# A decoder step with paged attention: weights turned and values issued one group later, maxima behind all four key pairs, two buffers for a sequence's values

## The reference

```python
ckv_past = cache_ckv[l, page_table].reshape(db, past_len, KV_LORA)
kr_past = cache_krope[l, page_table].reshape(db, past_len, MLA_ROPE)
...
s_past = (jnp.einsum('bthl,bpl->bhtp', q_lat, ckv_past)
          + jnp.einsum('bthr,bpr->bhtp', q_rope, krope_past))
...
p = jax.nn.softmax(s, axis=-1)
lat = (jnp.einsum('bhtp,bpl->bthl', p[..., :P], ckv_past)
       + jnp.einsum('bhts,bsl->bthl', p[..., P:], c_kv))
return jnp.einsum('bthl,lhv->bthv', lat, w_uv)
```

## Time and profile before

| | us |
|---|---|
| timed runs, median of 3 | 1979.57 |
| lowest, highest | 1977.12, 1981.09 |
| span of the profiled execution | 1973.4 |
| PE busy in it | 1875.2 (95%) |
| DVE, ACT, POOL busy | 1215.5, 567.5, 547.0 |
| paged stage, from DVE's first turned keys to the first output tile | 652.9 to 889.7 |

### The profile page before, as it was taken

How to read it: one execution, slowest core, us unless ns; L and a number is a source line. 1 busy time by engine, 2 the same in 40 slices (tenths; PEclk the granted TensorE clock), 3 DMA queues, 4 the chain that set the end, 5 groups by cost and what they waited for, 6 DMA issues and landing times.

```text
span 1973.4 us, 35022 instructions
## 1 busy us (share of the span) xinstructions
PE 1875.2 (95%) x15121; PEld 1617.4 (82%) x15121; DVE 1215.5 (62%) x1579; ACT 567.5 (29%) x962; POOL 547.0 (28%) x384
## 2 busy tenths in 40 slices
PE   7999999998899899999998699998999999999999
PEld 7988888884566444448997589998999999999998
DVE  5585583675677888875433746884377177375475
ACT  5222221244444455552121332110011011021026
POOL 2212211240000243423224013433333333333540
PEclk8999999998999999999999899999999999999999
DMA  7211211133000798943124402111211211211202
GB/s 237 53 46 33 55 45 33 30 74 120 1 1 1 293 339 329 337 172 129 33 86 150 160 22 65 43 43 34 64 44 34 63 43 33 65 38 38 86 22 89
DMA packets 162310, 176.77 MB, mean 90 GB/s; under 512 B 21982, under 2 KB 146932, under 8 KB 157772
## 3 DMA queue, kind: packets, MB, share of 16 engines
q1 hardware_dynamic: 146240, 93.54, 16.1%
q0 software_dynamic: 7168, 75.50, 10.0%
q10 hardware_dynamic: 8750, 5.49, 0.9%
HBM read 161.33 MB, written 13.27 MB: 88 GB/s over the span
## 4 chain that ended last, share of the span: by engine, by line
PE 79%; DVE 13%; ACT 4%; issue 2%; DMA 1%; POOL 1%; ACTq 0%; DVEq 0%; POOLq 0%; SPq 0%
PE PS L769 18%; PE PS L771 18%; PE PS L770 18%; PE PS L1060 4%; PE PS L806 4%; PE PS L1093 3%; PE PS L1001 2%; PE PS L850 2%; DVE ct L2366 2%; PE PS L979 2%; PE PS L1050 1%; PE PS L1075 1%; DVE Sst L1939 1%; DVE small L2126 1%; DVE ct L2386 1%
## 5 line engine op out<-in xcount | busy, mean ns | idle before, releaser
L715 POOL CAST whi<-wraw 128x1024 fp32r<-128x1024 f32 (+4 forms) x142 | 139.9, 985 | 1019.4 <-PE PS L771 905.7
L769 PE MATMUL PS<-BH,whi 128*128 128x344 f32 x1152 | 368.9, 320 | 0.0
L770 PE MATMUL PS<-BL,whi 128*128 128x344 f32 x1152 | 367.1, 319 | 0.0
L771 PE MATMUL PS<-BH,wlo 128*128 128x344 f32 x1152 | 367.0, 319 | 0.0
L717 POOL TENSOR_TENSOR wlo<-wraw,whi 128x1024 fp32r<-128x1024 f32 (+4 forms) x142 | 309.1, 2177 | 11.4
L770 PEld LDWEIGHTS PS<-BL,whi 128*128 128x128 f32 x1152 | 216.2, 188 | 0.5 <-issue 0.5
L769 PEld LDWEIGHTS PS<-BH,whi 128*128 128x128 f32 x1152 | 216.2, 188 | 0.5 <-issue 0.5
L771 PEld LDWEIGHTS PS<-BH,wlo 128*128 128x128 f32 x1152 | 216.2, 188 | 0.0
L769 PE MATMUL PS<-XH,whi 128*128 128x344 f32 x528 | 180.3, 341 | 3.4 <-DVE XL L1826 3.4
L2274 DVE TENSOR_TENSOR XT<-PS,XT 128x1032 f32<-128x1032 f32 x48 | 59.2, 1232 | 179.7 <-PE PS L771 179.6
L770 PE MATMUL PS<-XL,whi 128*128 128x344 f32 x528 | 169.6, 321 | 0.0
(11 more groups left out here) (445 smaller groups left out, 3729.3 us busy)
## 6 DMA issues: line engine op xcount, KB each, us to landing
wraw<-in_w_up_dram SPq DMA_DIRECT2D x44, 512.0 KB, 3.9
wraw<-in_w_in_dram SPq DMA_DIRECT2D x20, 512.0 KB, 4.1
wraw<-in_w_down_dram SPq DMA_DIRECT2D x24, 256.0 KB, 2.8
wraw<-in_w_down_dram SPq DMA_DIRECT2D x16, 320.0 KB, 3.1
xt_kept<-XT SPq DMA_DIRECT2D x1, 4128.0 KB, 13.4
XT<-xt_kept SPq DMA_DIRECT2D x1, 4128.0 KB, 13.5
xstage<-in_x_prompt_dram SPq DMA_DIRECT2D x8, 512.0 KB, 10.1
wraw<-in_w_out_dram SPq DMA_DIRECT2D x8, 512.0 KB, 4.7
```

Source lines behind the costliest of these rows:

```text
L715: gp.tensor_copy(hi, raw).then_inc(w_hi_done, 1)
L769: pe.matmul(out, wh[:, t, 0:m], hi[:, tile(t), s], start=(t == first), stop=False)
L770: pe.matmul(out, wh[:, t, 0:m], low, start=False, stop=False)
L771: ins = pe.matmul(out, wl[:, t, 0:m], hi[:, tile(t), s], start=False, stop=(t == last))
```

## The change

The turn of a group's weights and its values move one group later on PE: between key products g + 1 stands the turn of the weights of g - 1, and values g - 1 follow. The last two groups' turns and values stand behind the last sum. ACT follows: the copies of weights and values are those of g - 1, and the exponential of g comes at the end of the loop's turn, behind the copy of values g - 1. DVE turns all four pairs of g + 1 before it takes the maximum of g. `Og` has two buffers, one for even and one for odd sequences, so that values of a sequence may be copied out while POOL still reads those of the one before. The exponentials raise a counter of their own, `freed["ps"]`. Slots, key buffers, banks and the number of instructions of a group stay as they are; the gather of group g + 5 still waits for values g.

```diff
@@ -158,10 +158,12 @@
...
-        rc4, Og = place(V1, B1, ("rc4", [P, GP, KVL], F32), ("Og", [P, NG, KVL], F32))
+        rc4, Og1 = place(V1, B1, ("rc4", [P, GP, KVL], F32), ("Og1", [P, NG, KVL], F32))
+        Og = [Og0, Og1]
@@ -215,7 +217,7 @@
-        freed = {n: sem(f"freed_{n}") for n in ("v", "s", "rv", "rs")}
+        freed = {n: sem(f"freed_{n}") for n in ("v", "s", "ps", "rv", "rs")}
...
@@ -1063,8 +1069,8 @@
-                    if n == 2 and g:
-                        turn_weights(g - 1)
+                    if n == 2 and g > 1:
+                        turn_weights(g - 2)
@@ -1101,12 +1107,15 @@
                 if g + 1 < GT:
                     part_scores(g + 1)
                 else:
-                    turn_weights(g)
-                    pe.wait_ge(seq_w, NS)
-                    turn("m1", [nmS])
-                group_values(g)
+                    turn_weights(g - 1)
+                if g:
+                    group_values(g - 1)
                 if g + 1 < GT:
                     sum_scores(g + 1)
+            turn_weights(GT - 1)
+            pe.wait_ge(seq_w, NS)
+            turn("m1", [nmS])
+            group_values(GT - 1)
...
@@ -1612,28 +1621,36 @@
-            parts_out(0)
-            group_exp(0)
-            for g in range(GT):
+            def weights_out(g):
                 full(act, ("gpt", g))
                 if g >= 2:
                     full(act, ("go", g - 2))
                 copy_out(("gpt", g), PTs[g % 2][:, :, :].rearrange("p n k -> p (n k)"), bank(("gpt", g)))
+
+            def values_out(g):
+                b = g // NG
+                if g % NG == 0 and b > 1:
+                    act.wait_ge(seq_o, b - 1)
+                copy_out(("go", g), Og[b % 2][:, g % NG, :], bank(("go", g))[:, 0:KVL])
+
+            parts_out(0)
+            for g in range(GT):
+                if g:
+                    weights_out(g - 1)
                 if g + 1 < GT:
                     parts_out(g + 1)
...
+                if g:
+                    values_out(g - 1)
+                group_exp(g)
+                if g % NG == NG - 1:
+                    sequence_weights(g // NG)
+            weights_out(GT - 1)
...
+            values_out(GT - 1)
@@ -2214,13 +2231,11 @@
                 if g + 1 < GT:
                     turn_rope_keys(g + 1)
-                    for n in range(3):
+                    for n in range(4):
                         turn_key_pair(g + 1, n)
                 if g and g % NG == 0:
                     sequence_total(g // NG - 1)
                 group_max(g)
-                if g + 1 < GT:
-                    turn_key_pair(g + 1, 3)
@@ -2235,6 +2250,7 @@
             full(ve, ("go", GT - 2))
+            ve.wait_ge(seq_o, NS - 1)
             cat_low(0), cat_low(1)
```

More of the change, by code:

```diff
@@ L487, in build_program @@
         plan_parts(0)
-        use(("ps", 0), [4], "s")
+        use(("ps", 0), [4], "ps")
         for g in range(GT):
-            use(("gpt", g), [7], "s")
+            if g:
+                use(("gpt", g - 1), [7], "s")
             if g + 1 < GT:
                 plan_parts(g + 1)
[L493 to L496, removed]
+            if g:
+                use(("go", g - 1), [6], "s")
             if g + 1 < GT:
-                use(("ps", g + 1), [4 + (g + 1) % 2], "s")
+                use(("ps", g + 1), [4 + (g + 1) % 2], "ps")
+        use(("gpt", GT - 1), [7], "s")
+        use("m1", [4], "v")
+        use("m2", [0], "v")
+        use(("go", GT - 1), [6], "s")
         use("fin", [6, 7], "v")
@@ L690, in sequence_values @@
             emptied(eng, ("go", NG * b + NG - 1))
[L691 to L693 removed]
+            og = Og[b % 2]
+            step(eng.tensor_tensor(og[:, :, :], og[:, :, :], wgt.unsqueeze(2).broadcast_to([P, NG, KVL]), ALU.mult))
+            step(eng.tensor_tensor(og[:, 0:2, :], og[:, 0:2, :], og[:, 2:4, :], ALU.add))
+            eng.tensor_tensor(Oacc[:, b, 0:KVL], og[:, 0, :], og[:, 1, :], ALU.add).then_inc(seq_o, 1)
         @block.gpsimd
@@ L1132, in _ @@
             for g in range(NG):
-                pe.matmul(PS[r, k, 0:KVL], selW[:, g, :], Og[:, g, :], start=False, stop=False, skip_group_check=True)
+                pe.matmul(PS[r, k, 0:KVL], selW[:, g, :], Og[(NS - 1) % 2][:, g, :], start=False, stop=False, skip_group_check=True)
             for b in range(NS):
@@ L1621, in _ @@
                 copy_out(("gpt", g), PTs[g % 2][:, :, :].rearrange("p n k -> p (n k)"), bank(("gpt", g)))
+            def values_out(g):
[5 more added lines that the diff above has]
+            for g in range(GT):
+                if g:
+                    weights_out(g - 1)
                 if g + 1 < GT:
                     parts_out(g + 1)
-                else:
-                    cat_high(0), cat_high(1)
-                    act.wait_ge(c_new, 1)
-                    act.activation(wnew[:, 0:H], wnew[:, 0:H], ACT.Exp).then_inc(c_exp, 1)
-                    act.wait_ge(c_diff, 2)
-                    act.activation(fac, fac, ACT.Exp).then_inc(c_fac, 1)
-                if g % NG == 0 and g:
-                    act.wait_ge(seq_o, g // NG)
-                copy_out(("go", g), Og[:, g % NG, :], bank(("go", g))[:, 0:KVL])
-                if g + 1 < GT:
-                    group_exp(g + 1)
-                    if g % NG == NG - 2:
-                        sequence_weights(g // NG)
+                if g:
+                    values_out(g - 1)
[3 more added lines that the diff above has]
+            weights_out(GT - 1)
+            cat_high(0), cat_high(1)
+            act.wait_ge(c_new, 1)
+            act.activation(wnew[:, 0:H], wnew[:, 0:H], ACT.Exp).then_inc(c_exp, 1)
+            act.wait_ge(c_diff, 2)
+            act.activation(fac, fac, ACT.Exp).then_inc(c_fac, 1)
+            values_out(GT - 1)
             cat_high(2), cat_high(3)
```

9 lines of the change are left out of this document (5 added, 4 removed).

## The result

The changed kernel takes 1984.93 us (median of 11 runs) and the kernel before, beside it, 1977.99: a ratio of 1.0033, 95% interval 1.0019 to 1.0048, that is +3.8 to +9.5 us. The forecast was +3.7 us, and taking the ratio's middle the change costs +6.5. The profiled execution has a span of 1978.9 us, 5.5 more than the 1973.4 of before.

A forecast was written before the change was run, and what follows sets the result against it. The prediction took PE's own row to bound the paged stage, not waits for the softmax. Terms of 0 for steady groups, -1.0, +4.5 and +0.2 made +3.7 us, 1983.3 us, with a range of 1975.5 to 1990.5.

The forecast's parts named there:

- Steady groups: Middle of the paged stage: moving turn and values one group later gives nothing, covered by PE's 6.5 us per group; 0.
- The slack: Ordinary group: exponential's accumulator read 0.71 us before the turn's weight load, so the softmax chain is ready some 0.65 us early.
- First group: Start of the stage: no turn 0 or values 0 between key products 1 and sum 1; -1.0 us.
- Last group: End of the stage: output weights' load waits for later values 30, issued 3.5 us later than now; +4.5 in the sum.
- the lower clock: Sign of being wrong: PE at its lower clock after longer idle before the output tiles, adding to the tail.
- still end well before: End of the stage: first output tiles, some 3 us of matmuls, finish well before the second may start, 894.56 + 3.5.
- Gathers: Each gather issued one group later, running one group longer at the end, with 11.0 us left to land; +0.2 us.
- The rival of late pages: Gathers needing over 11.0 us make PE wait for key pairs in every group; +4 to +8 us, chance 0.17.
- The sum: Whole kernel: first group, last group and gathers together, -1.0 + 4.5 + 0.2 = +3.7 us, just inside 0.2% (4.0 us).
- The gaps and the supply of instructions: Gaps before the turn in 12 groups come from instruction supply through the same DMA engines, which the change leaves alone.
- The softmax rival: Ordinary groups: PE does wait for the exponential, so the change gives back 3.6 us, 14.7 with the gaps; chance 0.15.

The follow-up runs named there:

- the two repairs: Page 0's memory laid out in another order, in the kernel before (1976.66 us, ratio 0.999) and in the changed kernel (1981.97 us, ratio 1.0009).

## Why the prediction was right or wrong

**Steady groups, 0: right on the first kind of chip.** The 29 periods differ by 0.8 us, less than the gaps differ between two executions. The slack went from 0.71 to 2.04 us and nobody was waiting. The reason given, that the releaser named in the earlier trace rows is merely the last to come, is borne out by that (the smallest distance before is 0.53 us, not 0.55). It is not a property of the kernel alone: on three other chips the same chain is on the path.

**First group, -1.0: right**, -0.95.

**Last group, +4.5: right in its mechanism, 0.46 us short.** The load goes out at 884.52 (884.2 forecast), 3.85 us behind the sum's end (3.8 forecast). From there to the second output tile are 14.23 us, not 13.9: the four operations of the splits on POOL take 9.6 us instead of 9.0. What the prediction did not see is the branch beside the load, DVE's chain behind turn 31. It changed nothing in the sum, but together with the lower clock it is why the two repairs gave 1.90 and 1.63 us where I expected 3.5 and 4.3 to 4.7. The lower clock, which the prediction names as a sign of being wrong, did come in the changed kernel (from 893.7 to 897 us) and cost nothing: the first output tile ends at 898.3, and the second waits for POOL until 898.5. Of "still end well before" 0.4 us were left; this was luck.

**Gathers, +0.2: right in size**, as far as the gaps let one see. The prediction put a gather at 8.5 to 10.5 us against a margin of 11.0; where DVE waited for it, it read the pages 9.3 to 11.3 us after the request. For DVE that is too late by 1.2 us in 20 of the groups, which the prediction named as a sign of its rival. PE had enough of turned keys in hand. The rival of late pages is thereby out at this distance; at 4.8 us less it is real.

**The sum, +3.7: just under the interval's lower edge, +3.8.** The traces give +4.8 for the three parts, -0.65 ahead of them and +1.3 behind the stage, +5.5 of span in all. Of the 2.8 us between the forecast and the +6.5 of the timed runs, 0.46 are the tail and 0.6 the gaps, which differ by more than that between executions of like kernels; the rest has no cause that a run shows. The measured difference passes 0.2%, where I had put it just inside.

**The gaps and the supply of instructions: right on the first kind of chip.** The prediction held the gaps for the supply of instructions behind the gathers' traffic. The packets of the queue that carries instructions, 16 KiB each, bear that out. In the trace of before there are 11 places between groups 2 and 31 at which PE starts no matmul for 0.56 to 1.61 us, beside the regular pauses at turn and values. Every one of them ends 2.25 to 2.46 us behind the start of such a packet, and at the same place of PE's stream, its 193rd or 194th instruction when all that the trace has are counted in blocks of 256. The changed kernel has 11 as well, at places 193 to 195 and 2.24 to 2.51 us behind a packet. A group is 285 instructions of PE, 29 more than a block, so that the place moves through the group and is back after nine groups: this is the rhythm of the earlier trace rows. A gather's issue need not be under way, as a gap in the chain of before shows:

```profile
860.28 0.75 issue
```

The last gather is asked for at 853.00 and its second issue ends at 855.20; its pages arrive until 862.5. With the gathers left out (on the second kind of chip) the packets start over 150 instructions ahead of that place, where those before a gap start 30 to 112 ahead, and no gap is left. Whether it is the gathers' traffic or their issue that makes a packet late was not tested. The Trainium skill ("Runtime: NRT & Kernel Launch", Instruction fetch mechanics) says that the fetch is mostly hidden; the trace agrees, with 11 gaps for the 34 packets up to group 31, and none for 34 without gathers.

On the second kind of chip the loss is another: there PE's weight loads pause for 0.6 us at 0.7, 1.4 and 2.1 us behind the start of an issue, in every group of the changed kernel with a gather, wherever the block stands, and moving the issue moves the pauses.

**The softmax rival**, priced at 3.6 to 14.7 us, is right on the second kind of chip: 10.8 us.

## What to carry to other kernels

A step moved one round later is free in the middle only, and its price stands where the pipeline ends: follow what waits for the last rounds, and after the first branch ask how far behind the second one is. The releaser that a profile names is late only if it ends where the engine starts; measure that distance in every round. And a chain with little slack can be free on one chip and on the path on another: the sign of this change, +0.33% and -0.27%, depends on it. A gap without a releaser that comes back every nine groups wants to be counted in instructions and not in groups.

## What the runs showed of the hardware

On three chips PE was held back while POOL issued an indirect gather (two instructions of 0.94 us, 2.2 us in all): a completion that fell into it was seen by other engines 2.2 us after the matmul's end, and key matmuls beside it ran in bursts with 0.6 us between them. The kernel before takes 24 to 28 us longer on these chips. On the first kind of chip such a completion takes 0.01 to 0.08 us, and only some groups have gaps, such as the 1.35 us shown, each behind an instruction packet that starts late. What distinguishes the chips is not known.

A DVE step on 8x8 numbers, 0.15 us by itself, took 1.04 and 2.31 us beside POOL's cast and subtraction of 128x1024 numbers and ended with them. The cause was not tested.

With the last sum and values swapped PE stood idle for 4.36 us ahead of the first output tile, at 900.63, and then ran at the lower of its two clock levels (0.50 of full from 901 to 906 us), at 0.29 us a matmul; from 907 us the granted clock is 1.00 again and a matmul takes 0.16. In the changed kernel PE is idle for 4.39 us up to 893.72, and the granted clock is 0.66 on average from 893 to 898 us.
